# Encoder trunk on Trainium2: lag table and mix matrix of the state space batches with the lag outermost and the group innermost

## What is computed

```
def s5_mixer(u, ...):                       # 512 channels = 32 groups x 16 channels, 64 states per group
    ug = u.reshape(bsz, L, S5_GROUPS, S5_GROUP)
    y = (s5_direction(ug, ..., False) + s5_direction(ug, ..., True) + d * ug)
    y = gelu(y.reshape(bsz, L, S5_WIDTH))
    y = y * sigmoid(y @ w_glu)

def s5_direction(u, lam, step, b, c, reverse):
    lam_bar = exp(lam * step); b_bar = ((lam_bar - 1) / lam) * b
    bu = einsum('gpc,blgc->blgp', b_bar, u)
    states = scan of x[t] = lam_bar * x[t -+ 1] + bu[t]
    return einsum('gcp,blgp->blgc', c, states).real
```

## Time and profile before

| | |
|---|---|
| median of three runs | 2504.37 us |
| profiled execution | 2503.21 us, its span 2501.4 us |
| TensorE busy | 2440.4 us, 98% |
| VectorE busy | 1522.5 us, 61% |
| ScalarE busy | 1148.8 us, 46% |
| mean granted TensorE clock | 0.993 |
| DMA packets under 2 KB | 41568 of 109666 |

### The profile page before, as it was taken

One profiled execution on the slowest core, in us unless ns is written; L12 is line 12 of the kernel. 1 busy time (PEld: TensorE's weight loads), 2 busy tenths in 40 slices (PEclk: granted clock), 3 DMA queues, 4 the chain that ended last, 5 costly groups with the idle time before them and its releaser, 6 DMA issues.

```text
span 2501.4 us, 35331 instructions
## 1 busy us (share of the span) xinstructions
PE 2440.4 (98%) x14138; PEld 2070.0 (83%) x14138; DVE 1522.5 (61%) x2600; ACT 1148.8 (46%) x2010; POOL 0.2 (0%) x4
## 2 busy tenths in 40 slices
PE   9989799999999999999999999999999999999999
PEld 5888676778888999898778888778878888888887
DVE  8899657676656755564565446657885544533332
ACT  4332436354543655544454434446665443533422
POOL 0000000000000000000000000000000000000000
PEclk9999899999999999999999999999999999999999
DMA  5324632255322555344224323223334422432322
GB/s 193 96 71 96 199 108 86 85 172 190 110 68 93 175 182 184 110 135 127 79 74 160 118 81 121 76 85 104 92 93 144 127 79 92 142 101 93 101 93 93
DMA packets 109666, 289.24 MB, mean 116 GB/s; under 512 B 18912, under 2 KB 41568, under 8 KB 108224
## 3 DMA queue, kind: packets, MB, share of 16 engines
q1 hardware_dynamic: 99664, 260.57, 33.1%
q10 hardware_dynamic: 9840, 26.41, 3.3%
HBM read 265.35 MB, written 19.50 MB: 114 GB/s over the span
## 4 chain that ended last, share of the span: by engine, by line
PE 81%; DVE 11%; ACT 4%; DMA 2%; issue 2%; ACTq 0%; SPq 0%; DVEq 0%
PE ps L1455 65%; PE ps L342 2%; PE ps L1521 2%; PE ps L1546 2%; PE ps L338 2%; DVE wlo L1432 1%; PE ps L1564 1%; PE ps L1588 1%; DVE ps L1739 1%; DVE ps L1738 1%; DVE yP L1740 1%; ACT yP L1607 1%; DVE ringP L1810 1%; DMA vst<-mem_in 1%; DMA wraw<-wt 1%
## 5 line engine op out<-in xcount | busy, mean ns | idle before, releaser
L1455 PE MATMUL ps<-in_hP,whi 128*128 128x512 f32 x1336 | 540.2, 404 | 2.3 <-issue 1.6
L1427 ACT ACTIVATE whi<-wraw 128x1024 fp32r<-128x1024 f32 x430 | 452.1, 1052 | 196.2 <-PE ps L1455 129.2
L1432 DVE TENSOR_TENSOR wlo<-wraw,whi 128x1024 fp32r<-128x1024 f32 x431 | 523.0, 1217 | 4.5 <-ACT whi L1427 4.2
L1455 PE MATMUL ps<-in_hP,wlo 128*128 128x512 f32 x1336 | 522.0, 391 | 0.0
L1455 PE MATMUL ps<-in_lP,whi 128*128 128x512 f32 x1336 | 521.3, 390 | 0.0
L1455 PE MATMUL ps<-in_hS,whi 128*128 128x256 f32 x1088 | 318.6, 293 | 5.6 <-DVE x L1761 4.3
L1455 PE MATMUL ps<-in_lS,whi 128*128 128x256 f32 x1088 | 308.3, 283 | 0.0
L1455 PE MATMUL ps<-in_hS,wlo 128*128 128x256 f32 x1088 | 308.2, 283 | 0.0
L1455 PEld LDWEIGHTS ps<-in_hP,whi 128*128 128x128 f32 x1336 | 251.5, 188 | 63.8 <-issue 11.3
L1455 PEld LDWEIGHTS ps<-in_lP,whi 128*128 128x128 f32 x1336 | 251.8, 188 | 55.2 <-issue 5.0
L1455 PEld LDWEIGHTS ps<-in_hP,wlo 128*128 128x128 f32 x1336 | 251.5, 188 | 54.2
(11 more groups left out here) (486 smaller groups left out, 3675.6 us busy)
## 6 DMA issues: line engine op xcount, KB each, us to landing
wraw<-wt SPq DMA_DIRECT2D x432, 512.0 KB, 3.5
wraw<-wt ACTq DMA_DIRECT2D x17, 512.0 KB, 4.3
k_scratch<-region_P SPq DMA_DIRECT2D x16, 256.0 KB, 3.0
v_scratch<-vtmp SPq DMA_DIRECT2D x32, 128.0 KB, 3.0
x<-x_in SPq DMA_DIRECT2D x4, 768.0 KB, 7.0
mix_mem<-mem_in ACTq DMA_DIRECT2D x4, 512.0 KB, 8.0
x<-x_in ACTq DMA_DIRECT2D x1, 2048.0 KB, 12.8
region_S<-k_scratch ACTq DMA_DIRECT2D x2, 1024.0 KB, 5.4
```

The source lines that it names most:

```text
L1427: nc.scalar.activation(whi[:, (n + 3) % NHI, :, :], wraw[:, ws(n), :, :], ACT.Copy).then_inc(wh.sem, 1)
L1432: nc.vector.tensor_tensor(wlo[:, ws(n), :, :], wraw[:, ws(n), :, :], whi[:, (n + 3) % NHI, :, :].bitcast(F32), ALU.subtract).then_inc(wr.s ...
L1455: last = nc.tensor.matmul(ps[:, m % 2, 0:N[prod.g]], w_[:, k, :], x_[:, k, :], start=(k == 0 and j == 0), stop=(k == KT - 1 and j == 2))
```

## The change

The lag table becomes [lag, channel, group] in place of [group, lag, channel] on its 16 partitions, and the mix matrix [(output step, channel), group] in place of [group, (output step, channel)]. Eight consecutive lags of all eight groups are then one contiguous run of 1024 elements, in the table and in the matrix. `rt_g` is the table seen with the group first; ScalarE's copies and VectorE's additions go through it and touch elements 8 apart (32 B). TensorE's stationary operand for a group takes every eighth element. Sizes, number of instructions, their order and all waits stay.

```diff
-            mt = ubf[:, 2 * GB * P:3 * GB * P].rearrange("p (g c) -> p g c", g=GB)
+            mt = ubf[:, 2 * GB * P:3 * GB * P].rearrange("p (n g) -> p n g", g=GB)
...
-            rt = xf[0:GC, 4 * T:4 * T + GB * LAG * GC].rearrange("p (g n c) -> p g n c", g=GB, n=LAG)
+            rt = xf[0:GC, 4 * T:4 * T + GB * LAG * GC].rearrange("p (n c g) -> p n c g", g=GB, n=LAG)
+            rt_g = rt.rearrange("p n c g -> p g n c")
...
                 for s in range(lo, hi):
-                    eng.dma_start(mt[GC * s:GC * s + GC, :, :], rt[:, :, SC - 1 - s:2 * SC - 1 - s, :].rearrange("c g t d -> c g (t d)"))\
+                    eng.dma_start(mt[GC * s:GC * s + GC, :, :], rt[:, SC - 1 - s:2 * SC - 1 - s, :, :].rearrange("c t d g -> c (t d) g"))\
                         .then_inc(m_loaded.sem, 16)
...
-                    nc.tensor.matmul(o, mt[:, g, :], u2[b % 2][:, g, :], start=True, stop=False)
+                    nc.tensor.matmul(o, mt[:, :, g], u2[b % 2][:, g, :], start=True, stop=False)
...
-                nc.scalar.activation(rt[:, :, SC:LAG, :], lagf[:, :, 1:SC, :], ACT.Copy)
-                nc.scalar.activation(rt[:, :, 0:SC, :], lagb, ACT.Copy).then_inc(rt_copied.sem, 1)
+                nc.scalar.activation(rt_g[:, :, SC:LAG, :], lagf[:, :, 1:SC, :], ACT.Copy)
+                nc.scalar.activation(rt_g[:, :, 0:SC, :], lagb, ACT.Copy).then_inc(rt_copied.sem, 1)
...
-                dve_chain(nc.vector.tensor_tensor(rt[:, :, SC - 1, :], rt[:, :, SC - 1, :], lagf[:, :, 0, :], ALU.add))
-                nc.vector.tensor_tensor(rt[:, :, SC - 1, :], rt[:, :, SC - 1, :], dd[:, GB * b:GB * b + GB, :], ALU.add)\
+                dve_chain(nc.vector.tensor_tensor(rt_g[:, :, SC - 1, :], rt_g[:, :, SC - 1, :], lagf[:, :, 0, :], ALU.add))
+                nc.vector.tensor_tensor(rt_g[:, :, SC - 1, :], rt_g[:, :, SC - 1, :], dd[:, GB * b:GB * b + GB, :], ALU.add)\
                     .then_inc(rt_ready.sem, 1)
```

## The result

The changed kernel takes **2513.5 us** (median of six runs, 2512.49 to 2515.76) beside 2503.81 us for the kernel before in the same comparison. The ratio is 1.0037, 95% interval 1.0027 to 1.0047: slower by 9.7 us. The forecast was 2506, the range ended at 2513. The profiled execution took 2512.49 us, its span is 2510.7.

The account below looks back on a forecast made before the run. VectorE was taken as the stricter bound, the stage ending with its memory normalization after the memory loads. Clock falling (+3.3 us) and holding (+0.3) gave +1.8 on 2504.4: 2506 us, range 2499 to 2513 for 8 in 10.

Parts of the forecast that it names:

- Clock falls: Case where TensorE's clock drops ahead of y(1), which ends 0.9 us later; total +3.3 us, against +0.3 if it holds.
- second rival: Strided weight loads and copies cost their upper ends, 2.7 and 2.5 us, without any rate gain: 2515 us; chance 0.21.
- what moves this point moves the end one for one: Start of VectorE's memory normalization, at 259.50 us: any shift there shifts the end equally, the next stage starting behind a barrier.
- 0.6 us per batch: Gain taken for the mix matrix's eight transfers per batch, between 0 and 1.2 us from a higher rate.
- I take 1.4 us: Added cost per batch of ScalarE's two copies writing 32 B apart, chosen between 0 and 2.5 us.
- 1.2 us taken: Added cost per batch of TensorE's 16 strided weight loads for y, chosen between 0 and 2.7 us.
- y(2) ends +3.2: Batch 2 if the clock falls: TensorE's y product ends 3.2 us later than before.
- y(2) ends about where it does now: Batch 2 if the clock holds: table ready -0.5 us, matrix -1.1, and the end of y(2) nearly unmoved.
- Hidden, cover left 0.7 us: Batch 1: ScalarE's copies end at 150.6, before VectorE comes at 151.30, so their delay costs nothing.
- TensorE +0.9: Batch 2 if the clock falls: TensorE's work comes 0.9 us later, as y(1) ends that much later.
- matrix +2.0: Batch 2 if the clock falls: the mix matrix lands 2.0 us later, after a table ready 2.6 us later.
- The rival's point of decision: Second rival decides from about 3.2 us per batch of weight loads and copies together; the forecast took 2.6.

Follow-up runs that it names:

- The run in the destination's order: Changed kernel with ScalarE's two copies going through elements in destination order, writing contiguous runs and reading PSUM with a 512-byte step: 2504.43 us, ratio 1.0002 to before.
- the fours: Whole change with groups in fours innermost (step of 4 elements, 16 bytes; transfer pieces of 2048 bytes), against the kernel before: 2513.12 us, ratio 1.0036.
- TensorE's step alone: Kernel before with only TensorE reading the mix matrix at a step of 8 elements; table and transfers as they were: 2509.81 us, ratio 1.0016.
- changed, copies as before: Changed kernel with ScalarE's copies and VectorE's additions writing the lag table contiguously again: 2503.99 us, ratio 0.9997 to the kernel before.
- pairs: Whole change with groups in pairs innermost (step of 2 elements, 8 bytes; transfer pieces of 1024 bytes), against the kernel before: 2503.35 us, ratio 0.9996.

## Why the prediction was wrong

The step that failed is TensorE's clock ahead of y(2), in the branch "Clock falls", and with it the length of every y: the forecast left y(2) at the full clock, 5.64 + 1.2 = 6.8 us, and it took 10.46; y(0) to y(2) together grew by 9.9 us. The second term is the price of ScalarE's copies, 1.4 us per batch taken and 2.35 measured. Both reach the end as VectorE's waits for the copies, 12.2 us in place of 2.3. The forecast was 7.5 us short, and the range by 0.5. The sign stands in the prediction as its second rival, with a chance of 0.21 and 2515 us; that its number is so close is partly luck, since it has y(2) at the full clock too and makes up for it with 2.7 us for each y's loads, of which 2.0 were measured.

- **The bound: right at its end, not in what leads to it.** VectorE's normalization of the memory as the point that sets the end, and "what moves this point moves the end one for one": +9.42 there, +9.7 in the median. But the prediction has the memory loads wait for tile 16 on TensorE. In the changed kernel tile 16 ends 8.22 us later and the loads are issued 9.44 us later: ScalarE's copies and four issues of the matrix had become the later path.
- **The transfers: right in number, by luck.** 0.6 us per batch was taken; 0.6 and 0.8 measured in batches 1 and 2 (7.4 and 7.2 us from issue to y against 8.0), 1.6 in batch 3. It was taken as a higher rate, and batches 1 and 2 show next to none: from the last issue to its landing 5.14 and 4.98 us against 5.17 and 5.20. The issues were counted at nothing because of what stands behind them on their queues; but the last transfer of the batch waits for them itself, and 0.55 us of the gain in batch 1 and 0.54 in batch 2 are there. Four issues got shorter by 0.7 us on ScalarE and 1.0 on SyncE, against 1.1 forecast.
- **ScalarE's copies: sized too low.** "I take 1.4 us"; measured 2.35, nearly the upper end of 2.5. The nearest row, VectorE's write with a step at 1.3 ns per element, gave the right price, (2254 - 998) / 1024 = 1.23 ns; I went to the middle for a row that showed the step on the PSUM side. The run in the destination's order shows why that row was no evidence: the step costs where it is written, not where it is read.
- **The weight loads: sized too low at full clock, and not what lengthened y most.** 1.2 us taken, 2.0 measured at clock 1.00, and next to nothing at 0.50 (8 groups by 1.31 against 1.28 us).
- **The clock: the step that failed most.** It was weighed for y(1) alone, between falling and holding, while "y(2) ends +3.2" and "y(2) ends about where it does now" left y(2) at the full clock, and y(0) at +1.2. But a table that comes later leaves TensorE idle longer ahead of y(2) as well. The forecast's own terms say so: with "TensorE +0.9" and "matrix +2.0" the gap of 2.06 us becomes 3.2, as uncertain as the 3.0 ahead of y(1). Measured were 3.59 us, and y(2) ran at 0.50. y(0) grew by 3.35, y(1) by 1.71, y(2) by 4.82 us. The forecast also took over from the rows that a clock that has fallen comes back within y; with the step it never did. With the gaps ahead of y(1) and y(2) filled and the clock held over both, the loss is 5.8 in place of 9.7 us.
- **The slack of batch 1: right in kind, spent twice.** "Hidden, cover left 0.7 us": with 3.1 for y(0) and 2.2 for the copies in place of 1.2 and 1.4, the cover was gone and 2.0 us over.
- **The rival's point of decision, 3.2 us of both per batch: passed.** Measured 2.35 + 2.0 at full clock; where between 2.6 and this it lies, no run shows. Its chance was too small: the one row with a step in the state buffer pointed at the upper ends.

What is open: why the clock, once down, comes back within y with contiguous loads and not with the step. And when it falls at all: after the same 1.65 us of idleness ahead of y(0) it held in the fours and in two kernels with contiguous loads, and fell in the others, so the idle time alone doesn't decide. And why the transfers, worth 1.2 us alone, are worth 3.9 in the changed kernel: the normalization starts 2.6 us later without them, and the rest isn't accounted for.

## What to carry to other kernels

A layout that makes one transfer contiguous hands its step to every engine that writes or reads that buffer; price each of them, at the upper end when the only row with a step in that memory says so, and let the side of PSUM carry the step where there is a choice. Costs that share one slack are to be added before they are compared with it: beside long pieces TensorE's step cost nothing and the copies' step 3.9 us, and both together 9.7. Where an engine is late, ask for each later wait what it does to TensorE's clock, not only to its start. And where a chain is delayed unevenly, look again at which of its branches comes last at each join: here the memory loads went from waiting for TensorE to waiting for ScalarE's issues.

## What the runs showed of the hardware

- Step of a write into the state buffer, float32, ScalarE, 1024 elements on 16 partitions: contiguous 998 ns, 8 B 1066, 16 B 2058, 32 B 2254. Step of 512 B on the PSUM side: 999.
- Stationary operand of 128 x 128 float32 read with a step, shortest load: contiguous 186 ns, 8 B 193, 16 B 308, 32 B 312. At the lower clock a group of six passes took 1.31 us with the step of 32 B and 1.28 without.
- Eight transfers of 64 KB from 16 partitions to 16, in pieces of 4096 B in place of 512 B: four issues take 3.5 in place of 4.2 us on ScalarE and 2.8 in place of 3.8 on SyncE; from the last issue to its landing it is 5.1, 5.0 and 6.4 us in batches 1 to 3 against 5.2, 5.2 and 7.5.
- After 0.68, 0.99 and 1.20 us of idleness ahead of y(1) the clock stayed at 1.00; after 1.53 us (TensorE's step alone) and 3.20 us (changed) it fell. In the kernel before it stayed after 2.06 us, ahead of y(2); with the step it fell there after 1.48 us (changed, copies as before).
- Once the clock was down in a y product, it came back to 1.00 within it in all eleven cases with contiguous loads or pairs, and in none of seventeen with a step of 16 or 32 B.
